# Gate rows from single products, layer 1 opened block by block, and four smaller moves in a two-layer decoder trunk

## The reference

```python
for l in range(DEPTH):                       # DEPTH = 2
    mod = c_act @ ada_w[l] + ada_b[l]
    sh1, sc1, g1, sh2, sc2, g2 = jnp.split(mod, N_MOD, axis=-1)
    h = modulate(rms_norm(x, norm_mix_g[l]), sh1, sc1)
    y = hybrid_ab(...) if l % 2 == 0 else conformer_conv(...)
    x = x + g1[:, None, :] * y
    h = modulate(rms_norm(x, norm_ffn_g[l]), sh2, sc2)
    x = x + g2[:, None, :] * grouped_moe(h, ...)
return rms_norm(x, final_norm_g)
```

## Time and profile before

| | us |
|---|---|
| median of 3 runs | 1629.83 |
| lowest and highest | 1627.28, 1630.64 |
| the profiled execution's own time | 1626.12 |
| its span in the trace | 1624.0 |

### The profile page before, as it was taken

One profiled execution on the slowest core, in us unless ns is written; L12 is line 12 of the kernel. 1 busy time (PEld: TensorE's weight loads), 2 busy tenths in 40 slices (PEclk: granted clock), 3 DMA queues, 4 the chain that ended last, 5 costly groups with the idle time before them and its releaser, 6 DMA issues.

```text
span 1624.0 us, 16879 instructions
## 1 busy us (share of the span) xinstructions
PE 1503.7 (93%) x5185; PEld 804.1 (50%) x5186; DVE 854.6 (53%) x1474; ACT 353.8 (22%) x742; POOL 417.5 (26%) x673
## 2 busy tenths in 40 slices
PE   5989999998999899999979999999899899999991
PEld 3774544446886444444434334345588544444440
DVE  2454488664324433433427898999643633443343
ACT  3210000000122233233332000012141233333333
POOL 2100000000000466656510000213000146665650
PEclk9999999999999899999999999999899999999996
DMA  9636046664234689799475454454232589679846
GB/s 340 212 119 195 26 155 196 210 203 130 105 97 177 238 237 302 235 305 305 97 210 164 122 148 120 118 135 106 79 130 78 202 304 372 187 216 295 253 98 232
DMA packets 151219, 302.44 MB, mean 186 GB/s; under 512 B 17622, under 2 KB 101682, under 8 KB 142977
## 3 DMA queue, kind: packets, MB, share of 16 engines
q1 hardware_dynamic: 121696, 222.71, 41.1%
q0 software_dynamic: 21248, 65.40, 16.0%
q10 hardware_dynamic: 8224, 13.67, 2.3%
HBM read 248.56 MB, written 53.12 MB: 186 GB/s over the span
## 4 chain that ended last, share of the span: by engine, by line
PE 72%; DVE 15%; DMA 8%; issue 2%; ACT 2%; POOL 1%; SPq 0%; DVEq 0%; POOLq 0%; ACTq 0%
PE bank L1064 20%; PE bank L1224 19%; PE bank L1143 16%; PE bank L1239 10%; DVE R L1862 6%; DVE WX L1431 3%; DMA WX<-in_moe_w_gate 2%; PE bank L1332 2%; DMA R<-xn_scratch,TCUR 2%; DMA xsum_scratch<-R,TSUM 1%; PE bank L1047 1%; PE bank L1081 1%; DVE R L1408 1%; DMA WX<-in_moe_w_down 1%; DMA xsum_scratch<-R,TCUR 1%
## 5 line engine op out<-in xcount | busy, mean ns | idle before, releaser
L1064 PE MATMUL bank<-HTR,WX 128*128 128x512 f32 x1024 | 452.9, 599 | 5.8 <-DMA WX<-in_hyb_w_in 4.8
L1224 PE MATMUL bank<-WX,R 128*128 x784 | 350.1, 600 | 12.7 <-issue 6.6
L1064 PEld LDWEIGHTS bank<-HTR,WX 128*128 128x128 f32 x1024 | 192.7, 191 | 245.2 <-issue 238.4
L1224 PEld LDWEIGHTS bank<-WX,R 128*128 128x128 f32 x784 | 146.2, 191 | 183.5 <-issue 183.3
L1862 DVE SCALAR_TENSOR_TENSOR R<-R,PT 128x512 f32<-128x512 f32 (+18 forms) x288 | 231.2, 803 | 10.2
L1143 PE MATMUL bank<-WX,R 128*128 128x256 f32 x1024 | 230.8, 384 | 2.2 <-DVE R L1408 1.1
L659 POOL DMA_INDIRECT R<-xn_scratch,TCUR x204 | 200.6, 983 | 49.7 <-issue 41.1
L1143 PEld LDWEIGHTS bank<-WX,R 128*128 128x128 f32 x1024 | 194.3, 192 | 31.8 <-issue 2.8
L1239 PE MATMUL bank<-WX,R 128*128 x408 | 185.3, 597 | 4.0 <-DVE R L1674 4.0
L794 ACT ACTIVATE R<-R,MCT 128x128 f32<-128x128 f32 x408 | 162.0, 481 | 19.6 <-DVE R L1658 19.6
L1685 DVE SCALAR_TENSOR_TENSOR R<-bank,GSLOT,HTR 128x512 f32<-128x512 f32 x51 | 38.3, 751 | 207.4 <-DMA xsum_scratch<-R,TSUM 156.4
(11 more groups left out here) (223 smaller groups left out, 1100.7 us busy)
## 6 DMA issues: line engine op xcount, KB each, us to landing
WX<-in_ada_w SPq DMA_DIRECT2D x48, 1024.0 KB, 11.8
WX<-in_moe_w_gate SPq DMA_DIRECT2D x32, 1024.0 KB, 5.6
WX<-in_moe_w_up SPq DMA_DIRECT2D x32, 1024.0 KB, 8.9
WX<-in_moe_w_down SPq DMA_DIRECT2D x32, 1024.0 KB, 13.9
WX<-in_conf_w SPq DMA_DIRECT2D x20, 1024.0 KB, 9.4
WX<-glu_scratch SPq DMA_DIRECT2D x64, 260.0 KB, 4.6
WX<-in_hyb_w_in SPq DMA_DIRECT2D x10, 1024.0 KB, 11.9
xsum_scratch<-WX ACTq DMA_DIRECT2D x8, 1024.0 KB, 5.4
```

Source lines behind the costliest of these rows:

```text
L1064: ins = pe.matmul(dst[:], lhs(k), rhs(k), start=(k == 0), stop=(k == kc - 1))
L1224: ins = pe.matmul(hid, XT[:, k, :], WXP[:, bass.ds(at, 2), k, :], start=(k == 0), stop=(k == KC - 1))
```

## The change

- **Gate rows.** TensorE reduces a gate row with one product of 256 columns. GpSimd loads the bias row into the slot beforehand, and VectorE adds the sum to it. The slot's semaphore now counts the load and the store.
- **Layer 1 opened by blocks.** ScalarE takes a root for each of blocks 0 to 3, after an early table load (`root_table`); VectorE scales each as it comes; TensorE transposes six k of each block at once into six banks, then the last two k. The first product waits for each k by itself. Fillers go from 20 to 15 products.
- **Constants.** The router's constants are made ahead of the last logits' copy.
- **Last squares.** For blocks 6 and 7 the first three quarters are squared between the evictions of pieces (3, 2) and (3, 3), the last quarter after.
- **Tile 1 peeled.** Its code stands ahead of the loop, and its register reads and weight waits ahead of the first hidden transposes.
- **Last taps moved.** `conv_taps(15)` goes from behind (0, 1) to behind (0, 2), the sums from (0, 2) to (0, 3), with the pieces (0, 0) to (0, 2) placed around `total(1, 0)`.
- **Last norm.** The root's table is loaded before the reload.

```diff
@@ GpSimd
+            def gate_bias(q):
+                l, s = q // 8, (2, 5)[q // 4 % 2]
+                c = s * D + q % 4 * QW
+                pool.dma_start(BROW[q % NBROW], i["ada_b"][l:l + 1, c:c + QW]).then_inc(brow_out[q % NBROW], 16)
+            for q in range(NBROW):
+                gate_bias(q)
...
                 pool.dma_start(g_dram[...], BROW[q % NBROW]).then_inc(brow_out[q % NBROW], 16)
+                if 1 <= q <= 16 - NBROW:
+                    pool.wait_ge(brow_out[(q - 1) % NBROW], 32 * ((q - 1) // NBROW) + 32)
+                    gate_bias(q - 1 + NBROW)
@@ ScalarE
+            def root_table():
+                link(act.activation(SD[:, 0:1], EPSC[:], ACT.Sqrt))
+            def block_root(b, reloads, done):
+                act.wait_ge(x_back[b], 16 * reloads)
+                link(act.activation(JUNK, X[:, b, :], ACT.Square, accum_out=SS[:, b:b + 1]))
+                act.activation(SD[:, b:b + 1], SS[:, b:b + 1], ACT.Sqrt, bias=EPSC[:], scale=1.0 / D).then_inc(done, 1)
...
+                        if (p, j) == (3, 2):
+                            act.wait_ge(xpj, 16 * l + 15)
+                            for b in (6, 7):
+                                link(act.activation(JUNK[:, 0:3 * QW], X[:, b, 0:3 * QW], ACT.Square,
+                                                    accum_out=SS[:, b:b + 1]))
+                            link(act.activation(SD[:, 6:8], SS[:, 6:8], ACT.Identity, bias=EPSC[:], scale=1.0 / D))
...
-            rms_sums(2, 0)
+            root_table()
+            for b in range(4):
+                block_root(b, 1, fin_sd if b < 3 else rms_sd)
@@ TensorE
-                    for c in range(2):
-                        o = dst[0:1, P * c:P * c + P]
-                        col = COL_ADAB + 48 * l + 8 * s + 2 * (g % 4) + c
-                        pe.matmul(o, ONES[:, 0:1], ACC[n % 2][:, P * c:P * c + P], start=True, stop=False)
-                        ins = pe.matmul(o, PT[:, col:col + 1], IDENT[:], start=False, stop=True)
+                    ins = pe.matmul(dst[0:1, 0:QW], ONES[:, 0:1], ACC[n % 2], start=True, stop=True)
...
+            def transposes_by_block():
+                def one(k, b):
+                    return pe.transpose(turn_bank(2, 0, k)[:, P * b:P * b + P], XN1[0][:, b, P * k:P * k + P], IDENT[:])
+                pe.wait_ge(tev_a, 8)
+                pe.wait_ge(tev_d, 8)
+                for b in range(4):
+                    pe.wait_ge(xn_ok, 16 + b + 1)
+                    for k in range(6):
+                        ins = one(k, b)
+                        if b == 3:
+                            ins.then_inc(tr, 1)
+                for k in (6, 7):
+                    pe.wait_ge((tev_a, tev_d)[k % 2], 9)
+                    for b in range(4):
+                        ins = one(k, b)
+                    ins.then_inc(tr, 1)
...
                 gates()
+                pe.wait_ge(tab_ok, l + 1)
+                nt = pe.value_load(RT[0:1, 0:1], min_val=2, max_val=MOST)
+                at1 = pe.snap(weights_of(expert_of(1)))
                 transpose_hidden(0)
-                pe.wait_ge(tab_ok, l + 1)
-                nt = pe.value_load(RT[0:1, 0:1], min_val=1, max_val=MOST)
-                with pe.Fori(1, nt) as t:
-                    gate_up(t, expert_of(t))
+                gate_up(1, at1)
+                down(0, 0)
+                transpose_hidden(1)
+                with pe.Fori(2, nt) as t:
+                    gate_up(t, weights_of(expert_of(t)))
...
-            keep_warm(20)
-            transposes(2, 0)
+            keep_warm(15)
+            transposes_by_block()
...
-                if (p, j) == (0, 1):
+                if (p, j) == (0, 2):
                     conv_taps(NSTEP - 1)
-                if (p, j) == (0, 2):
+                if (p, j) == (0, 3):
                     mean_quarters(1)
+                    x_piece(1, 0, 0)
                     total(1, 0)
+                    x_piece(1, 0, 1)
+                    x_piece(1, 0, 2)
@@ VectorE
-                    dve.tensor_copy(BROW[q % NBROW], src[0:1, 0:QW]).then_inc(ada_fin, 1)
+                    dve.wait_ge(brow_out[q % NBROW], 32 * (q // NBROW) + 16)
+                    tt(BROW[q % NBROW], src[0:1, 0:QW], BROW[q % NBROW], ALU.add).then_inc(ada_fin, 1)
...
+            def block_apply(b):
+                dve.wait_ge(*((fin_sd, b + 1) if b < 3 else (rms_sd, 5)))
+                link(dve.reciprocal(RSTD[:, b:b + 1], SD[:, b:b + 1]))
+                dve.tensor_scalar(XN1[0][:, b, :], X[:, b, :], RSTD[:, b:b + 1], None, ALU.mult).then_inc(xn_ok, 1)
...
+                route_constants()
                 logits_out(l, 3)
```

97 lines of the change are left out of this document (60 added, 37 removed).

## The result

The changed kernel took 1603.15 us (median of 4 runs, 1598.42 to 1605.76) against 1628.85 us (4 runs, 1627.28 to 1630.64): a ratio of 0.9846, 95% interval 0.9827 to 0.9865, that is 25 us faster. Five more runs later gave 1605.23 us (1602.62 to 1607.14), ratio 0.9859 [0.9837, 0.9880]. The forecast was 1607.6 with a range of 1600 to 1617. The profiled execution took 1605.76 us with a span of 1603.8, against a span of 1624.0 before: 20.2 us less, where the forecast's sum was 22.2.

A forecast was written before the change was run, and what follows sets the result against it. TensorE, busy 93% of the span, was taken to bound the kernel. The terms 6.5 + 1.7 + 2.7 + 1.8 + 7.2 + 2.3 + 0 = 22.2 us came off 1629.83, giving 1607.6 us, range 1600 to 1617.

The forecast's parts named there:

- Gate rows: Gate rows on TensorE: 15 rows on the chain save 0.43 us each, 6.5 us; bias loads cost nothing; bounds 5 to 7.5.
- Routing: End of each layer's projection: sigmoid 0.87 us earlier through constants, squares and roots; 1.7 us for two layers, bounds 0.5 and 2.2.
- Peel: Tile 1 of both layers' experts: less idleness before its product, 2.7 us, and half the clock loss regained, 1.8 us.
- Opening: Start of layer 1: first product 8.2 us earlier, less 1.0 for the clock, 7.2 us; bounds 4.7 and 9.1.
- Border: Last taps, last projection: shifted-row wait goes, but TensorE idles 6.9 us for third product's weights; gain 2.3, bounds 0 and 4.5.
- rival 1: Border before the last projection's third product: its weights arrive in time, border gives 10.6 us, total 1599.3 us; chance 0.08.
- Tail: Last norm: root's table load of 1.28 us leaves the chain, but DMA sets the end; gain 0, bounds 0 and 1.3.
- Rival 2: Clock and sequencer take the unproven half: opening 4.7, peel 0.4, no clock back in expert stages; 1614.2 us; chance 0.22.
- Rivals 3, 4 and 5: 3: opening hidden, 1614.8 us, chance 0.06; 4: bias loads slow it, 1655 us, 0.03; 5: nothing measurable, 1629.8 us, 0.03.

The follow-up runs named there:

- rows_four_products: Changed kernel with each gate row again made from four small products and a plain copy, bias rows still loaded but not added: 1609.80 us, ratio 0.9903 to the kernel before.
- opening_back: Changed kernel with layer 1's old opening: one root over four blocks, transposes after all four, 20 fillers: 1616.45 us, ratio 0.9937 to the kernel before.
- weights_early: Changed kernel with SyncE issuing the last projection's last two weight items ahead of the last shifted half: 1596.36 us, ratio 0.9815 to the kernel before.

## Why the prediction was right, and where it wasn't

The forecast of 22.2 us met 20.2 in the profile and 23 to 26 in the medians. One pair of traces is a thin measure where half clock falls now here, now there. This table sets the forecast beside the pair and beside the means over the traces of this case that have the edit and those that have not (number of traces in brackets):

| stretch | forecast | pair | without the edit | with it | means apart |
|---|---|---|---|---|---|
| gate rows: start of layer 0's logits | 6.5 | 4.3 | 460.4 (4) | 454.5 (10) | 5.9 |
| routing: logits to first expert product, both layers | 1.7 | 2.5 | 65.2 (3) | 65.9 (8) | -0.7 |
| peel: first expert to first down product, both layers | 4.5 | 5.6 | 38.3 (3) | 32.8 (11) | 5.5 |
| opening: fillers to first product | 7.2 | 9.9 | 29.1 (4) | 20.2 (10) | 8.9 |
| border: taps to product (1,0) | 2.3 | 0.7 | 51.1 (4) | 49.5 (8) | 1.6 |

**Gate rows, 6.5 forecast.** 0.44 us each against 0.43, no wait for a bias load (median landing 4.2 us). The mechanism and the size of one row are right. The stage shows 4.3 in the pair, 4.9 in rows_four_products and 5.9 between the means; the medians show 8.

**Routing, 1.7 forecast.** 2.5 in the trace, but not as forecast: this is the step that failed, in layer 0. I worked out the sigmoid's time, and it came 0.46 us earlier against the last-but-one eviction, half of the 0.87 forecast, and nearly all of that (0.41) was the constants' work. (The recorded working has a small slip: the logits' 2.6 us behind an eviction at 510.8 end at 513.4 and not at 513.25. VectorE would then be done at 514.05, just as the table load, so the 0.87 stands.) But I had written off the late last eviction as a delay of 0.74 that the logits absorb. It was 0.82, and it cost TensorE its clock: the fillers, which the forecast's chain left out, became the last wait in seven of the eight traces that have both the split and eight fillers. In the pair layer 0 gained 0.1 and layer 1 gained 2.4, of which 1.0 is up to the counts product, near the 0.87 forecast, and 0.7 is a filler row at a better clock (5.42 us for 8 instead of 6.15). Both numbers are luck of the trace: in six of the eight traces layer 0 takes 34.7 us here against 32.3 before, a loss, and over both layers the change's routing edits lost 0.7 us where 1.7 was forecast.

**Peel, 2.7 and 1.8 of clock forecast.** 2.9 and 2.7 measured. 2.2 of it is idle time, a little less than the 2.7, and 3.4 the clock, nearly all of the 3.6 that I had halved. The mechanism is right and the clock's term was too small. Both directions were shown, by taking it away and by giving it alone. The queue depth of 64 that the Trainium skill states ("TensorE: Matmul & The Clock Gate", the section on the array's architectural detail) is shown by no run here. That the sequencer makes the register reads while TensorE still works off the first product fits the idle time that is left, 0.7 to 0.8 us in the changed kernel's trace.

**Opening, 7.2 forecast with 9.1 as the bound.** 9.9 in the pair, of which 9.1 is from the fourth block's square on. The other 0.9 is not the edit's: the reload was issued no earlier (7.3 us after the fillers' start, before 7.1), but the fourth block's square began 7.6 us after that issue instead of 8.7, and in opening_back, with the old opening, it was 8.0. That trace puts the edit at 9.2, and the means at 8.9. The 1.0 us that I took off for the clock was wrong: it stayed at 1.00 through the transposes and the product. I had weighed a rule of the Trainium skill there ("TensorE: Matmul & The Clock Gate", "What's actually happening"), that the throttled clock is the default; in this trace it wasn't what came. Blocks coming one by one left TensorE idle for 0.4 to 0.7 us at once, not for 4.14 as before. The upper bound, 9.1, was the right number.

**Border, 2.3 forecast.** The wait was forecast at 6.9 us ahead of the third product and was 6.81, released by the weight load. The product took 10.2 us instead of the 8.7 forecast, so the gain was 0.7 in this trace; it was 1.5 in the trace with 9.4 (rows_four_products) and 2.2 in the one with 8.6 (opening_back). So the mechanism is right, and the size was the third product's time at half clock. That the order on SyncE's queue is the cause is shown by weights_early. It also confirms the price of rival 1, whose condition did not hold here: the border without the wait gives 10.8 us against before.

**Tail, 0 forecast.** 0.3, within the spread of the traces. **Not forecast:** 3.1 us lost in the two expert stretches, 1.7 of them one product at half clock, which the changed kernel's second trace does not have.

**Rivals.** Rival 2, the clock taking the unproven half, went the other way in the peel and the opening, and came true in the routing, where I hadn't put it. Rivals 3, 4 and 5 fell with the first trace. The sum was near in part by luck. In the pair its errors offset each other: 4.9 us too little for the opening, the peel, the routing and the tail; 3.8 too much for the rows and the border, and 3.1 that no term had. By the means, rows, peel and border are right within 1 us, the opening is 1.7 too small and the routing 2.4 too large.

## What to carry to other kernels

When a wait is removed, look at what the same queue issues behind it: moving the taps was worth 0.7 to 2.2 us, issuing the weights earlier nothing, and both together 10.8. The profile of before had named both: the wait for the shifted rows, and the weights issued behind them. Fillers that are to keep the clock must be counted at half clock too, since then they end late and become the wait themselves; and an eviction put back by 0.8 us can cost more in clock (1.6 to 3.3 us of the stretch behind it, in seven of eight traces) than the work that it made room for. Where single runs of the same code differ by 9 us, take the size of an edit from the distance between two instructions that enclose it, in several traces, and the median only for its sign.

## What the runs showed of the hardware

- At tile 1 the clock's fall went with the idle time without exception. 1.8 to 2.2 us of idleness were followed by a product of 8.55 to 8.83 us in all six cases (three traces with the loop, two layers each), and 0.5 to 1.1 us by one of 7.13 in all 22 cases with the peel. At the logits of layer 0, 1.50 us instead of 0.69 went with half clock in the fillers behind in nine of ten traces, and 0.69 in none of four.
- Yet the idle time alone does not decide. The tenth of those traces (rows_four_products) had the 1.50 us and kept the clock. In layer 1, 0.98 us at the same place were followed by fillers at full clock in five of the ten traces with split squares, and by fillers that lost 1.7 us at half clock in the other five (8.81 us for 16 or 5.38 for 8, instead of 7.11 and 3.68). The last down product of layer 0, behind the same 2.02 us in all fourteen traces, took 3.7 us in eight and 5.39 in six. What decides there stays open.
- The same code spread over 8.7 us in nine runs, with a mean granted clock between 0.974 and 0.980; the fastest run (1598.42) has the 0.980.
- A function table load for the root or the sigmoid took 1.28 us each time. Nothing stood between it and the function behind it where that was ready: in the kernel before, the load at 837.09 was followed by the root at 838.38.
